# The first stage of a three-layer kernel: loads in another order, four output units advanced together, bias table loads spread over the units

## The reference

```python
mod = silu(c) @ ada_w[layer] + ada_b[layer]          # and mod_c from c_ctx; 6 parts of 1024
sh1, sc1, g1, sh2, sc2, g2 = split(mod, 6)
xm = rmsnorm(h,  norm_g[layer, 0]) * (1 + sc1)  + sh1    # 256 latent tokens
cm = rmsnorm(hc, norm_g[layer, 0]) * (1 + sc1c) + sh1c   # 256 context tokens
pl, pc = xm @ w_in, cm @ w_in                            # 1024 x 2560
# columns 0:256 -> a 2-D Fourier transform; 256:2560 -> q, k, v of 12 heads of 64
# neighborhood attention: scores + bias from the table rpb, masked by column, softmax, @ v
```

## Time and profile before

| what | value |
|---|---|
| median of 3 runs | 1907.16 us (1902.48 to 1910.19) |
| profiled execution | 1909.19 us, its span 1907.4 us |
| mean granted clock of TensorE | 0.949 |
| busy in the span | PE 1740.3, DVE 1122.2, ACT 981.7 us |
| first unit product | 46.87 us |
| end of the last of the 22 units | 164.7 us |
| the 16 bias table issues | from 47.9 to 70.1 us |

### The profile page before, as it was taken

How to read it: one execution, slowest core, us unless ns; L and a number is a source line. 1 busy time by engine, 2 the same in 40 slices (tenths; PEclk the granted TensorE clock), 3 DMA queues, 4 the chain that set the end, 5 groups by cost and what they waited for, 6 DMA issues and landing times.

```text
span 1907.4 us, 27379 instructions
## 1 busy us (share of the span) xinstructions
PE 1740.3 (91%) x11008; PEld 1444.8 (76%) x11008; DVE 1122.2 (59%) x1496; ACT 981.7 (51%) x1288; POOL 71.1 (4%) x68
## 2 busy tenths in 40 slices
PE   5999989699999879999878879999959989999898
PEld 2786665588888648889656668888948988887588
DVE  2440664699889674343231288988955584634464
ACT  3322663488888544224321268888844572344362
POOL 0000000100000100000000010000010000100100
PEclk8999999799999979999889989999979998999899
DMA  8626004799999863224244469999964444264521
GB/s 333 159 89 236 30 1 185 290 393 410 408 402 406 340 239 133 89 88 176 90 176 177 154 247 405 403 413 405 397 241 149 180 152 159 64 202 156 133 67 68
DMA packets 52979, 421.73 MB, mean 221 GB/s; under 512 B 17028, under 2 KB 18180, under 8 KB 30608
## 3 DMA queue, kind: packets, MB, share of 16 engines
q1 hardware_dynamic: 26272, 364.55, 48.9%
q0 software_dynamic: 8592, 32.69, 5.5%
q10 hardware_dynamic: 18016, 23.07, 3.6%
HBM read 399.27 MB, written 21.02 MB: 220 GB/s over the span
## 4 chain that ended last, share of the span: by engine, by line
PE 82%; DVE 9%; ACT 3%; DMA 3%; issue 2%; POOL 1%; DVEq 0%; SPq 0%; ACTq 0%; POOLq 0%
PE ps L693 43%; PE ps L828 18%; PE ps L650 7%; PE ps L673 2%; PE ps L839 1%; PE ps L700 1%; PE ps L684 1%; DMA arena<-xtok_d,slot_tok 1%; DMA arena<-y_d,tok_row 1%; PE ps L1228 1%; PE ps L846 1%; PE ps L1073 1%; PE ps L1044 1%; DMA hT<-h 1%; PE ps L1059 1%
## 5 line engine op out<-in xcount | busy, mean ns | idle before, releaser
L2078 DVE TENSOR_TENSOR w_lo<-ring,w_hi 128x1024 fp32r<-128x1024 f32 x384 | 452.7, 1220 | 58.6 <-ACT w_hi L1519 56.8
L1519 ACT ACTIVATE w_hi<-ring 128x1024 fp32r<-128x1024 f32 x384 | 396.0, 1057 | 102.6 <-PE ps L828 58.6
L693 PE MATMUL ps<-XT_lo,arena_r 128*128 128x256 f32 (+1 forms) x1712 | 386.9, 301 | 10.0 <-DVE ring_r L1948 7.2
L693 PEld LDWEIGHTS ps<-XT_lo,arena_r 128*128 128x128 f32 x1712 | 283.0, 191 | 25.8 <-issue 7.9
L828 PE MATMUL ps<-w_hi,x_hi 128*128 128x256 f32 (+1 forms) x768 | 250.0, 325 | 4.9 <-issue 4.8
L828 PE MATMUL ps<-w_hi,x_lo 128*128 128x256 f32 (+1 forms) x768 | 246.0, 320 | 0.0
L828 PE MATMUL ps<-w_lo,x_hi 128*128 128x256 f32 (+1 forms) x768 | 245.7, 320 | 0.0
L693 PE MATMUL ps<-arena_r 128*128 128x512 f32 (+1 forms) x624 | 226.1, 362 | 13.2 <-DVE ring_r L2302 7.0
L1948 DVE TENSOR_TENSOR ring_r<-ring,arena_r 128x1024 fp32r<-128x1024 f32 x96 | 113.7, 1223 | 123.6 <-ACT arena_r L1421 123.4
L693 PE MATMUL ps<-XT_lo,ring_r 128*128 128x256 f32 x640 | 180.4, 282 | 0.0
L828 PEld LDWEIGHTS ps<-w_hi,x_hi 128*128 128x128 f32 x768 | 146.8, 191 | 21.3 <-issue 6.0
(11 more groups left out here) (336 smaller groups left out, 2569.2 us busy)
## 6 DMA issues: line engine op xcount, KB each, us to landing
ring<-w_all SPq DMA_DIRECT2D x172, 2048.0 KB, 9.4
y_d<-arena ACTq DMA_DIRECT2D x32, 512.0 KB, 10.0
arena<-toep_d POOLq DMA_DIRECT2D x16, 384.0 KB, 9.4
arena<-rpb ACTq DMA_DIRECT2D x16, 192.0 KB, 5.4
xtok_d<-arena ACTq DMA_DIRECT2D x6, 512.0 KB, 2.7
hT<-h SPq DMA_DIRECT2D x1, 2048.0 KB, 12.8
arena<-cb_d POOLq DMA_DIRECT2D x1, 1536.0 KB, 9.3
arena<-cc_d POOLq DMA_DIRECT2D x1, 959.0 KB, 6.3
```

The lines of the kernel that those rows point to most:

```text
L693: last = nc.tensor.matmul(out, a, b, start=(first and i == 0), stop=(final and i == 2))
L1519: nc.scalar.activation(w_hi[:, q], slot(b, "p (q c) -> p q c", q=4)[:, q], ACT.Copy).then_inc(hi_rdy, 1)
L2078: nc.vector.tensor_tensor(w_lo[:, q], slot(base + n, "p (q c) -> p q c", q=4)[:, q], as_f32(w_hi[:, q]), ALU.subtract).then_inc(*split_sig ...
```

## The change

- **Loads.** hT comes first, in two halves with a semaphore each, then cst, then blocks 0, 1, 2. Block order: ada blocks 0 and 2 (shift and scale for k 0 to 3), mix block 0, ada 1 and 3, then mix blocks 1 to 4.
- **Norm.** VectorE adds the squares 0 to 6 (`norm_partial`), TensorE makes two ones-products (`norm_part`) instead of eight. ScalarE loads the Sqrt table before it waits for hT.
- **Gains** are made in two halves, after each scale block; `mod_ready` counts one more from there on.
- **Units 0 to 3 together.** k is the outer loop: at each k three products for each of four units, in four banks. Mix block 0 is split in eight half pieces (four units x k 0 to 3 and 4 to 7), the lo parts into memory of their own. The rows of the second pair of ada blocks and the release of the slot come at k = 2, their columns at k = 3.
- **Bias table loads.** One after the copy of each of units 0 to 15. VectorE splits pieces 5 to 18 first, then waits for the sixteen loads, makes the first mask pair, splits piece 19, and makes the second pair.

```diff
-ADA_CUTS = (0, 4, 8, 13, 16, 24)
+ADA_CUTS = (0, 2, 4, 8, 13, 16, 24)
 ADA_BLOCKS = [range(a, b) for a, b in zip(ADA_CUTS, ADA_CUTS[1:])]
 B_ADA0 = 0
-B_MIX = B_ADA0 + 4
-B_ADA1 = B_MIX + 5
+B_MIX0 = B_ADA0 + 2
+B_ADA0B = B_MIX0 + 1
+B_MIX1 = B_ADA0B + 2
+MIX_AT = (B_MIX0, *range(B_MIX1, B_MIX1 + 4))
+MOD_ORDER = (0, 2, 1, 3)
+B_ADA1 = B_MIX1 + 4
...
@@ -428,11 +433,21 @@
 
         def mix_part(p, of):
 
-            n = B_MIX + p // 4
+            n = MIX_AT[p // 4]
             if 14 <= p < 16:
                 s = of[:, (n % SLOTS) * BLK:(n % SLOTS + 1) * BLK].rearrange("p (k m) -> p k m", k=KT)
                 return s[:, 4 * (p - 14):4 * (p - 14) + 4, SEQ:2 * SEQ]
             return part_of(n, p % 4, p >= 16, of)
+
+        def mix_lo(p):
+
+            if p < 4:
+                return area_r(3072 + 1024 * p, 1024).rearrange("p (k m) -> p k m", k=KT)
+            return mix_part(p, ring_r)
+
+        def mix_half(j):
+
+            return j % 4, slice(4 * (j // 4), 4 * (j // 4) + 4)
 
         def mix_free(p):
 
...
@@ -562,11 +577,11 @@
         @block.sync
         def _(sp):
             sp.dma_start(sm[:, :], smalls).then_inc(ld_sm, 16)
+            sp.dma_start(hT[:, 0:4], h0[:, 0:4]).then_inc(ld_h, 16)
+            sp.dma_start(hT[:, 4:KT], h0[:, 4:KT]).then_inc(ld_h2, 16)
+            sp.dma_start(cst[:, :], cst_d).then_inc(ld_cst, 16)
             for j in range(SLOTS):
                 sp.dma_start(slot(j), w_all[j]).then_inc(w_full[j], 16)
-                if j == 0:
-                    sp.dma_start(cst[:, :], cst_d).then_inc(ld_cst, 16)
-                    sp.dma_start(hT, h0).then_inc(ld_h, 16)
 
             holds = {B_MOE0 + 1: (x_st, 64), B_ADA3 + 2: (y_st[0][1], 128), B_RET: (f_cmb, 3), B_IB + 1: (y_st[1][1], 128), B_Z1: (f_cmb, 6)}
...
                 a, b = NORM_COLS[i]
-                pe.wait_ge(nm_part, (i + 1) // 2)
+                pe.wait_ge(nm_part, (1, 2, 0, 3)[i])
                 nc.tensor.matmul(ps[:, 7, 0:b - a], ones, squares_of(i)[:, 0], start=True, stop=False)
                 norm_sum(i, KT - 1)
 
@@ -976,24 +991,35 @@
             pe.wait_ge(c2_ready, 1)
             pe.wait_ge(tick_ready, 1)
             pe.sem_inc(split_used, 3)
-            mod_rows_of(0, 0)
             pe.wait_ge(ld_cst, 16)
+            norm_part(0)
+            for a in (0, 1):
+                mod_rows_of(a, 4 + a)
+                mod_cols_of(a, 6 + a, after=1 + a)
             for k in range(KT):
-                norm_sum(0, k)
-            for a in range(1, 4):
-                mod_rows_of(a, a % 2)
-                mod_cols_of(a - 1, 2)
-            mod_cols_of(3, 2)
-            unit = 0
-            for b in range(5):
+                pe.wait_ge(nm_lo, k + 1)
+                if k == 2:
+                    mod_rows_of(2, 4)
+                    mod_rows_of(3, 5)
+                    pe.wait_ge(dw_lo, 8)
+                    release(MIX_AT[0])
+                if k == 3:
+                    mod_cols_of(2, 6, after=2)
+                    mod_cols_of(3, 7, after=2)
+                for unit in range(4):
+                    if k == 0:
+                        pe.wait_ge(dw_lo, unit + 1)
+                    last = three_terms(ps[:, unit, :], mix_hi(unit)[:, k], mix_lo(unit)[:, k], mix_x[:, k], XT_lo[:, k],
+                                       k == 0, k == KT - 1)
+                    if k == KT - 1:
+                        last.then_inc(mx_mm, 1)
+            unit = 4
+            for b in range(1, 5):
                 for m in range((4, 4, 4, 2, 0)[b]):
-                    if unit >= 4:
-                        pe.wait_ge(mx_ev, unit - 3)
-                    pe.wait_ge(dw_lo, unit + 1)
-                    w, w2 = mix_hi(unit), mix_part(unit, ring_r)
+                    pe.wait_ge(mx_ev, unit - 3)
+                    pe.wait_ge(dw_lo, DW_MIX + unit + 1)
+                    w, w2 = mix_hi(unit), mix_lo(unit)
                     for k in range(KT):
-                        if unit == 0:
-                            pe.wait_ge(nm_lo, k + 1)
                         last = three_terms(ps[:, unit % 4, :], w[:, k], w2[:, k], mix_x[:, k], XT_lo[:, k], k == 0, k == KT - 1)
                     last.then_inc(mx_mm, 1)
                     unit += 1
@@ -1005,12 +1031,12 @@
                         for k in range(KT):
                             p = first + k // each
                             if tt == 0 and k % each == 0:
-                                pe.wait_ge(dw_lo, p + 1)
+                                pe.wait_ge(dw_lo, DW_MIX + p + 1)
                             last = three_terms(ps[:, unit % 4, 0:1024 // each], mix_x[:, k, toks], XT_lo[:, k, toks],
-                                               mix_hi(p)[:, k % each], mix_part(p, ring_r)[:, k % each], k == 0, k == KT - 1)
+                                               mix_hi(p)[:, k % each], mix_lo(p)[:, k % each], k == 0, k == KT - 1)
                         last.then_inc(mx_mm, 1)
                         unit += 1
-                release(B_MIX + b)
+                release(MIX_AT[b])
             pe.wait_ge(mx_ev, unit)
 
 
...
                 if p % 4 == 0:
                     act.wait_ge(w_full[n % SLOTS], 16 * (n // SLOTS + 1))
                 if mix_free(p):
                     act.wait_ge(*mix_free(p))
                 nc.scalar.activation(mix_hi(p), mix_part(p, ring), ACT.Copy).then_inc(dw_hi, 1)
 
+            def mix_early(j):
+
+                p, k = mix_half(j)
+                if j == 0:
+                    act.wait_ge(w_full[MIX_AT[0] % SLOTS], 16 * (MIX_AT[0] // SLOTS + 1))
+                nc.scalar.activation(mix_hi(p)[:, k], mix_part(p, ring)[:, k], ACT.Copy).then_inc(dw_hi, 1)
+
+            def bias_rows(r, kr):
+
+                act.dma_start(bias_na[(r % 2) * GRID_W:(r % 2 + 1) * GRID_W, r // 2, :, kr * GRID_W:(kr + 1) * GRID_W],
+                              bass.AP(tensor=rpb.tensor,
+                                      offset=(kr - r + NA_KH - 1) * RPB_W + NA_KW - GRID_W,
+                                      ap=[[1, GRID_W], [RPB_HEAD, NA_H], [1, GRID_W]])).then_inc(ld_rpb, 16)
+
+            table(ACT.Sqrt)
             act.wait_ge(ld_h, 16)
             for k in range(KT):
+                if k == 4:
+                    act.wait_ge(ld_h2, 16)
                 norm_square(0, k)
             norm_root(0)
-            for a in range(4):
-                rows_out(a, a % 2)
-            mix_split(0)
-            act.wait_ge(mod_ready, 1)
+            rows_out(0, 4)
+            rows_out(1, 5)
+            mix_early(0)
             for k in range(KT):
+                act.wait_ge(mod_ready, 1 + k // 4)
                 act.wait_ge(nm_tmp, k + 1)
                 for seg in range(2):
                     toks = slice(seg * SEQ, (seg + 1) * SEQ)
                     last = nc.scalar.activation(mix_x[:, k, toks], XT[:, k, toks], ACT.Identity, scale=gains[:, 0, k, seg:seg + 1],
                                                 bias=modc[:, 0, k, seg:seg + 1])
                 last.then_inc(nm_x, 1)
-            for p in range(1, 5):
-                mix_split(p)
-            for r in range(ROWS):
-                for kr in range(ROWS):
-                    act.dma_start(bias_na[(r % 2) * GRID_W:(r % 2 + 1) * GRID_W, r // 2, :, kr * GRID_W:(kr + 1) * GRID_W],
-                                  bass.AP(tensor=rpb.tensor,
-                                          offset=(kr - r + NA_KH - 1) * RPB_W + NA_KW - GRID_W,
-                                          ap=[[1, GRID_W], [RPB_HEAD, NA_H], [1, GRID_W]])).then_inc(ld_rpb, 16)
+                if k == 0:
+                    for j in range(1, 4):
+                        mix_early(j)
+                if k == 3:
+                    for j in range(4, 8):
+                        mix_early(j)
+                    rows_out(2, 4)
+                    rows_out(3, 5)
+            mix_split(4)
             for u in range(22):
                 act.wait_ge(mx_mm, u + 1)
                 if u < 2:
@@ -1650,6 +1694,8 @@
                     mix_split(u + 5)
                 elif u == 17:
                     mix_split(19)
+                if u < 16:
+                    bias_rows(u // ROWS, u % ROWS)
             for n, (seg, f) in enumerate((s, f) for s in range(2) for f in range(2)):
...
+                if a in (1, 3):
+
+                    dve.wait_ge(mt_ev, a + 1)
+                    half_k = slice(m - 8, m - 4)
+                    nc.vector.scalar_tensor_tensor(
+                        gains[:, 0, half_k], modc[:, 0, m:m + 4], 1.0,
+                        sm[:, SM["norm_g"]][:, half_k].unsqueeze(2).broadcast_to([P, 4, 2]), ALU.add, ALU.mult
+                    ).then_inc(mod_ready, 1)
+                elif a % 6 == 3:
 
                     dve.wait_ge(mt_ev, a + 1)
...
             dve.wait_ge(ld_cst, 16)
             nc.vector.tensor_copy(tok_bf[:, :], cst[:, CST["tok"]])
+            dve.wait_ge(nm_std, 1)
```

(60 more changed lines are left out.)

24 lines of the change are left out of this document (13 added, 11 removed).

## The result

| | before | after |
|---|---|---|
| median of the runs | 1907.58 us (4 runs, 1902.48 to 1910.19) | 1886.45 us (4 runs, 1885.82 to 1888.68) |
| ratio | 1 | 0.9895 [0.9872, 0.9917] |
| profiled execution (span) | 1909.19 (1907.4) | 1885.98 (1884.2) |
| mean granted clock | 0.949 | 0.955 |

The front did what the forecast said: the mix stage (the 22 projection units) ends 13.35 us earlier, 13.8 were forecast. The rest came behind it, where nothing was to change in length.

What follows compares the result with a forecast made beforehand. TensorE was taken to carry 82% of the chain of waits. Units 0 to 3 ending 15.9 us earlier, less a 2.1 us stall, gave 13.8 us less: 1893.4 us predicted, with 1888 to 1902 holding some 8 in 10.

Steps and rivals of the forecast that it cites:

- Loads, norm, modulation, start of the units: Front: block 2 lands at 24.7, norm products end at 15.3, gains at 24.0, first unit product at 28.4, before 46.87.
- Half clock on the first products: Units' start: TensorE, idle before, begins at half rate; twelve products at k = 0 take 4.6 us.
- rows and columns: Second pair of ada blocks, between k = 1 and k = 3: rows 3.9 us, columns 2.1.
- Next block, copies: Mix block 1 lands at 47.7, before unit 4 needs it at 58.6; four PSUM copies, 0.6 + 1.05 each, hidden.
- Bias loads: Unit 18: mix_split(19) behind VectorE's wait for all sixteen loads opens a new TensorE stall of 2.1 us, ends 0.5 and 3.5.
- L: Time from the end of unit 15 until the last bias load lands, taken as 4.0 us.
- nobody waited: In before, sixteen bias-load issues held ScalarE's queue until 70 us, with no engine waiting for it.
- the tail gap: Rival: the bias-load gap also drops TensorE to half rate, 1.4 + 1.9 us more, 1896.7; chance 0.13.
- the sparse work in the middle: Rival: rows and columns between k = 1 and k = 3 at half rate, 3.4 + 1.6 us more, 1898.4; chance 0.10.
- half clock through all four units: Rival, 28 to 58 us: clock stays at 0.50, 22.1 us more with rows and columns, 1915.5; chance 0.04.
- given back: Rival: a later stage paced by something that doesn't move swallows most of the gain, 1900 to 1907; chance 0.07.
- Everything behind 165 us is released by events and should move as one: Behind the mix stage: all stretches keep their length, so the front gain passes whole to the end.

Runs made afterwards that it cites:

- a_biasold: after with its 16 bias loads put back ahead of the copies instead of one behind each: 1909.31 us in one run.
- b_shift3: before, started later by two VectorE memsets that hold SP's loads back: 1912.51 us (10 runs).
- a_shift13: after, started later by six VectorE memsets that hold SP's loads back (delay 13.8): 1902.26 us (9 runs).
- b_pad: before with twelve tiny unread TensorE products added ahead of its norm sums: 1904.21 us (10 runs).
- a_pad: after with twelve tiny unread TensorE products added ahead of the norm: 1892.51 us (4 runs).
- a_ones8: after with TensorE summing the eight squares in eight ones-products again, VectorE adding none: 1894.83 us (5 runs).
- a_padend: after with the twelve tiny products farther back, run at 1592.8 us in its trace: 1888.62 us (4 runs).
- a_hold: after with hT asked for behind block 0 and cst, as in before: 1897.94 us in one run.
- r_after2: after unchanged, profiled a third time: 1886.56 us.

## Why the forecast was right in front and wrong behind

- *Loads, norm, modulation, start of the units*: right, each within 0.5 us.
- *Half clock on the first products*: right in kind. I had the first 24 products at 7.4 us in all; they took 8.47 in the first profile of after, where the clock stayed at 0.50 until 34 us, and 7.2 and 8.1 in the two others, so the term lies within what executions of one kernel show. With rows and columns a little under their terms (3.64 for 3.9, 1.84 for 2.1) the fourth unit ends at 59.70 instead of 58.6.
- *Next block, copies*: right, hidden. *Bias loads*: right mechanism; L was 3.4 instead of 4.0 and the stall 1.28 instead of 2.1. The two errors nearly cancel: 13.35 us in the first profiles (13.7 between the medians of three) against 13.8. That "nobody waited" for ScalarE's queue was true of before only, and a_biasold shows the price of it behind the new front, 15.3 us.
- *Rivals*: no lower clock behind the tail gap (the 78 products behind it took 18.30 us, 0.235 each); the sparse work in the middle ran at full clock (rows 3.64 for 32, the rate of the earlier trace rows); no half clock through all four units; nothing given back.
- **The step that failed**: "Everything behind 165 us is released by events and should move as one." The sum took nothing off behind the mix stage, without testing it, and there it was mis-sized: by the medians of three profiles each it shrank from 1739.5 to 1733.7, 5.8 us (9.8 in the first pair, which the drawn levels made look larger). The table says where. 165 to 1434 is 1266.7 in both medians: no gain. 1434 to 1796 went from 361.5 to 358.3, **3.2 us**, in all three profiles of either kernel. It does not hang on time: b_shift3 and a_shift13 keep their kernel's value at another time. Twelve tiny products ahead turn it round in both directions: b_pad has the value of after, a_pad and a_ones8 that of before; put behind the place of the wait (a_padend) they don't. For 2.6 of the 3.2 us, those in 1434:1616, this holds in every kernel of the table to 0.3 us. They belong to where TensorE's instructions come to stand in the program, and the change, which adds and removes products in front, moved them as a pad does: it makes twelve products fewer on record ahead of the place, and a_pad and a_ones8 bring back exactly the count of before. The other 0.6 us, in 1616:1796, go the same way in the pads, but a_hold and a_biasold show 180.55 and 181.36 with TensorE's program unchanged, so place is not their only cause, and it stays open.
- 1796 to the end mostly shows 111.3 or 108.7 (four variants of after lie at 112.0, 111.7, 110.1 and 109.6): in before always the first (3 of 3), in after once the first and twice the second. The profiles with 181 in 1434:1616 all show 111.2 to 111.4. Whether the two are linked or this is drawn with unequal odds stays open; it is worth 0 to 2.6 us.
- The sum: 13.7 in front, 3.2 in 1434:1796, up to 2.6 at the end, make 16.9 to 19.5 of the 21.1 in medians; the three profiled executions of each differ by 19.6 (medians 1906.17 and 1886.56). What is left of 21.1, 1.6 us or somewhat more, is within what the four runs of after leave uncertain (0.22% of 1907 is 4.2 us). Likewise of a_pad's 6.0 us only 3.1 are found in 1434:1796; most of the rest, 2.7 against r_after2, is at the end.

The pads show that the wait follows the number of TensorE instructions ahead of the place, and the shifts that it does not follow the time; whether their place in the program counts or how many have been executed, no run here can tell apart. That TensorE waits there for a packet of its program is an inference from one constant delay, 1.26 to 1.46 us from the packet's end in six traces; no run moved the packet alone.

## What to carry to other kernels

Work out the changed stage from its waits, as far as its events reach; but when a change adds or removes instructions on the engine that bounds, allow some 3 us either way for stretches far behind that it doesn't touch, and look there for a wait ascribed to "issue", or to an engine that had long been done, in the midst of work whose operands are ready, and count the instructions ahead of it in both kernels. Before an early start is claimed, ask of each queue that was idle by luck: here sixteen loads, free ahead of a stage that was late, would have cost 15 us ahead of one that is early. Profile an unchanged kernel two or three times before a stretch's 1 to 3 us are put down to an edit, for the profile that is at hand may show either level.
